# A two-layer hybrid attention trunk on one core: gates' Silu behind the eviction, output banks freed by the copy, gating by two heads of four row tiles, first weights from ScalarE's queue, indexer keys in eights

## What is computed

```python
h = rmsnorm(x, norm_pre)
q, k, v, qi, ki, wi, ga, xb, gb, u, vc, gc = split(h @ w_in)
ya = sparse_attention(...)          # indexer scores relu(qi.ki) weighted by wi, top-k keys, softmax, values
yb = pool_mix(xb)                   # causal windows 2, 4, 8, 16, then a small product and a scale
vn = layernorm(vc); yc = u * (tril(sgu_w[h]) @ vn + sgu_b[h])   # four heads h, chunks of 128 rows
y  = concat([ya * silu(ga), yb * silu(gb), yc * silu(gc)])
x  = x + rmsnorm(y @ w_out, norm_post)
```

## Time and profile before

| | |
|---|---|
| three runs | 1000.95 us median (998.19 to 1001.85) |
| profiled execution | 999.5 us, of which 997.8 us span |
| TensorE (PE) busy | 934.6 us, 94% |
| VectorE (DVE) busy | 535.9 us, 54% |
| ScalarE (ACT) busy | 305.4 us, 31% |
| granted TensorE clock | 0.994 of full speed on average |

### The profile page before, as it was taken

How to read it: one execution, slowest core, us unless ns; L and a number is a source line. 1 busy time by engine, 2 the same in 40 slices (tenths; PEclk the granted TensorE clock), 3 DMA queues, 4 the chain that set the end, 5 groups by cost and what they waited for, 6 DMA issues and landing times.

```text
span 997.8 us, 20531 instructions
## 1 busy us (share of the span) xinstructions
PE 934.6 (94%) x7100; PEld 483.7 (48%) x7100; DVE 535.9 (54%) x1718; ACT 305.4 (31%) x674; POOL 272.6 (27%) x484
## 2 busy tenths in 40 slices
PE   5798999999999999998999999999999999999996
PEld 3434444444454555554555444444445455555543
DVE  4336999475883233233444499966678623332232
ACT  3121121432124245423231211225212424543312
POOL 8710232232222211413342013223222222241110
PEclk9899999999999999999999999999999999999998
DMA  9841677576866655856584338766677667566551
GB/s 314 166 134 43 211 265 250 187 245 226 295 212 212 240 191 186 305 165 222 149 246 128 110 105 280 249 226 207 244 262 246 198 214 249 167 229 247 170 179 53
DMA packets 91954, 205.21 MB, mean 206 GB/s; under 512 B 15047, under 2 KB 26550, under 8 KB 91858
## 3 DMA queue, kind: packets, MB, share of 16 engines
q0 software_dynamic: 38944, 123.98, 36.5%
q1 hardware_dynamic: 47778, 75.78, 23.2%
q10 hardware_dynamic: 5136, 4.20, 1.5%
HBM read 193.88 MB, written 10.14 MB: 204 GB/s over the span
## 4 chain that ended last, share of the span: by engine, by line
PE 74%; DMA 8%; ACT 5%; DVE 4%; issue 4%; ACTq 3%; SPq 1%; POOL 0%; POOLq 0%; DVEq 0%
PE bank L1490 36%; PE bank L1847 10%; PE bank L1507 5%; PE bank L1542 5%; DMA pg<-in_cache_k_dram 4%; PE bank L1473 4%; ACTq L624 2%; PE bank L1723 2%; DMA pg<-in_cache_v_dram 2%; PE bank L1759 2%; PE bank L1591 2%; DMA r<-in_x_prompt_dram 2%; PE bank L1649 1%; PE bank L1565 1%; DVE r L1399 1%
## 5 line engine op out<-in xcount | busy, mean ns | idle before, releaser
L1490 PE MATMUL bank<-wr,ht 128*128 128x512 f32 (+1 forms) x1024 | 436.2, 579 | 5.3 <-DVE ht L1198 2.0
L1490 PEld LDWEIGHTS bank<-wr,ht 128*128 128x128 f32 x1024 | 190.8, 191 | 219.2 <-issue 202.7
L705 POOL DMA_DIRECT2D wr<-in_w_in_dram x50 | 37.1, 742 | 293.0 <-PE bank L1490 225.2
L722 POOL DMA_DIRECT2D pg<-in_cache_v_dram x128 | 69.8, 546 | 165.1 <-PE bank L1542 121.3
L722 POOL DMA_DIRECT2D pg<-in_cache_k_dram x128 | 69.5, 543 | 83.3 <-PE bank L1507 59.2
L1116 DVE TENSOR_SCALAR_CACHE_REDUCE r<-r,sel_i 128x1088 bf16<-128x1088 f32 x62 | 82.8, 1336 | 0.0
L1507 PE MATMUL bank<-pg,qbx 128*32 128x256 f32 x1024 | 63.4, 383 | 7.6 <-DMA pg<-in_cache_k_dram 4.2
L1473 PE MATMUL bank<-wr,ht 128*32 128x256 f32 (+1 forms) x1152 | 65.2, 379 | 2.9 <-DMA wr<-in_w_in_dram 2.6
L1542 PE MATMUL bank<-pg,rs 128*32 128x256 f32 x1024 | 62.3, 382 | 1.8 <-DMA pg<-in_cache_v_dram 1.8
L1847 PE MATMUL bank<-wr,qt 128*128 128x512 f32 x128 | 58.4, 599 | 1.8 <-ACT rs L923 1.8
L1847 PE MATMUL bank<-wr,ht 128*128 128x512 f32 x128 | 57.5, 592 | 0.0
(11 more groups left out here) (271 smaller groups left out, 1167.3 us busy)
## 6 DMA issues: line engine op xcount, KB each, us to landing
pg<-in_cache_k_dram SPq DMA_DIRECT2D x128, 256.0 KB, 5.0
pg<-in_cache_k_dram POOLq DMA_DIRECT2D x128, 256.0 KB, 5.8
pg<-in_cache_v_dram SPq DMA_DIRECT2D x128, 256.0 KB, 5.0
pg<-in_cache_v_dram POOLq DMA_DIRECT2D x128, 256.0 KB, 5.8
wr<-in_w_in_dram POOLq DMA_DIRECT2D x40, 512.0 KB, 4.2
wr<-in_w_in_dram POOLq DMA_DIRECT2D x6, 1024.0 KB, 6.0
...
```

The costliest lines, as they stand in the source:

```text
L705: pool.dma_start(W[n % 2][:, k, d0:d0 + w], src[k.start * P:k.stop * P, c0:c0 + w].rearrange("(k p) n -> p k n", p=P))\
L722: pool.dma_start(PG[2 * gi + e], cache[l, bass.ds(nos[2 * gi + e], 1), :, :].rearrange("o p n -> p (o n)"))\
L1490: mm = pe.matmul(b[0:m, 0:w], HT[:, k, rt * P:rt * P + m], W[n % 2][:, k, 0:w], start=(k == 0), stop=(k == KC - 1))
```

## The change

- **First weights.** ScalarE's own queue issues the weights of chunk kg (two DMAs) before anything else; then it takes one Sqrt of a dummy value, which loads the table that both Square and Sqrt use. GpSimd issues its first 8 keys, waits for these weights, and then issues chunk qi and the constants. The identity's DMA now brings the rotation tables and `query` too, and the cast of the selectors moves to step `wt`.
- **Keys in eights.** A key step of SP and GpSimd loads 8 page numbers and issues 8 DMAs; ScalarE's loads 4 and issues 4. Who brings which keys is dealt anew, and TensorE waits for even and odd quarters apart. On SP tile 2 of x now stands behind 8 keys and tile 3 behind another 8.
- **Order.** `kis` and `whx` go from slot 4 to slot 2; `qis` stays at slot 4 but ahead of that slot's rotation. Chunk q's weights are one DMA behind slot 6. In slots 27, 30, 31, 37 and 39 to 41 `L` goes behind `V`/`K` and `PV`. The last two mask pieces of pair 2 go from slot 30 to the end of slot 29, behind `turn`. `gT` of tiles 1 and 2 go one and two slots back, a `turn` moves from slot 22 to slot 23. `res` and `norm` go to BACK, where they stand behind the key steps of the same slot.
- **Banks.** Chunk xg is copied whole and its bank given back; Silu follows from SBUF behind `P` and `P2`. `out` gives its bank back after the copy, and squares the copy in SBUF.
- **Gating.** `sg` takes two heads of all four prompt tiles at once: two groups of 2 heads x 256 columns in slots 32 and 33.
- **The end.** For the last tile the product with `norm_post` is taken ahead of the root, half by half (`og`), so that one operation is left behind it.

```diff
-KEY_STEPS = [("keys", 1, pair, j) for pair in (0, 1) for j in range(NCH)]
-POOL_KEYS = [("pool keys", 1, pair, j) for pair in (2, 3) for j in range(NCH)]
-TURNS_AT = ((20, 0, 0, (0,)), (20, 4, 0, (1,)), (21, 4, 0, (2,)), (22, 4, 0, (4, 3)),
+SP_KEYS = (((2, 0), (2, 2), (3, 0), (3, 2), (2, 1), (2, 3), (3, 1)), ((2, 0), (3, 0), (2, 2), (3, 2), (2, 1), (3, 1), (2, 3), (3, 3)))
+POOL_KEYS = (((0, 0), (0, 2), (1, 0), (0, 1), (0, 3), (1, 1)), ((0, 0), (0, 2), (0, 1), (0, 3)))
+ACT_KEYS = (((1, 2), (3, 3), (1, 3)), ((1, 0), (1, 2), (1, 1), (1, 3)))
+KEY_STEPS = [[("keys", pair, j, u) for pair, j in ACT_KEYS[l] for u in range(2)] for l in range(DEPTH)]
+def keys_asked(queue, l, odd):
+    return sum(8 for n in range(l + 1) for _, j in queue[n] if j % 2 == odd)
+LOGITS_FIRST = (25, 26, 28, 32, 33, 34, 35, 36, 38)
+TURNS_AT = ((20, 0, 0, (0,)), (20, 4, 0, (1,)), (21, 4, 0, (2,)), (22, 4, 0, (3,)), (23, 0, 0, (4,)),
             (27, 4, 1, (0,)), (29, 4, 1, (1,)), (30, 4, 1, (2,)), (31, 4, 1, (4, 3)),
             (36, 4, 2, (0,)), (37, 4, 2, (1,)), (38, 0, 2, (2,)), (39, 4, 2, (4, 3)),
             (40, 4, 3, (0,)), (41, 4, 3, (1,)), (42, 4, 3, (2,)), (43, 4, 3, (4, 3)))
-MASKS_AT = ((0, (18, 4), (19, 0), 19), (1, (20, 0), (20, 4), 21), (2, (29, 4), (30, 0), 30), (3, (36, 4), (37, 0), 37))
+MASKS_AT = ((0, (18, 4), (19, 0), 19), (1, (20, 0), (20, 4), 21), (2, (29, 0), (29, 4), 30), (3, (36, 4), (37, 0), 37))
...
-        for n, s in zip((1, 2, 2, 3, 3, 4), KEY_STEPS):
-            put(n, BACK, s[:1] + s[2:])
+        for n, s in zip((1, 2, 2, 3, 3, 4), KEY_STEPS[0]):
+            put(n, BACK, s)
...
+    put(at["kg", ST] + 2, FRONT, ("kis",), ("whx",))
+    put(at["qi", ST] + 1, FRONT, ("qis",))
-    put(at["qi", ST] + 1, FRONT, ("kis",), ("whx",), ("qis",))
...
+    for rt in RTP:
+        put(at["xg", rt], ROWS_A, ("silu", "xg", rt))
...
-        put(n, ROWS_A, ("L", i, c))
+        put(n, ROWS_A if n in LOGITS_FIRST else ROWS_B, ("L", i, c))
...
-    for n, rt in enumerate(RTP):
-        put(33 + n, COLS if rt == ST else FRONT, ("sg", rt))
+    put(32, FRONT, ("sg", 0))
+    put(33, FRONT, ("sg", 1))
+    put(37, COLS, ("sg", ST))
+    for rt in RTP:
...
-    for i, n in enumerate((35, 37, 40, 44)):
+    for i, n in enumerate((35, 38, 42, 44)):
...
-            put(46 + n, BACK, KEY_STEPS[n][:1] + KEY_STEPS[n][2:], layer=l + 1)
-        for s, n in zip(POOL_KEYS, (45, 45, 46, 46, 47, 48, 49)):
-            put(n, BACK, s[:1] + s[2:], layer=l + 1)
+            put(46 + n, BACK, KEY_STEPS[l + 1][n], layer=l + 1)
+            put(45 + n, BACK, ("pool keys",) + POOL_KEYS[l + 1][n], layer=l + 1)
     last = {rt: n_out + max(m for m, o in enumerate(OUTS[l]) if o[0] == rt) for rt in RTP}
     for rt in RES[l]:
-        put(last[rt], ROWS_B, ("res", rt))
+        if l + 1 == DEPTH and rt == ST:
+            for j in range(2):
+                put(last[rt] - 1 + j, BACK, ("og", rt, j))
+        put(last[rt], BACK, ("res", rt))
         if l + 1 < DEPTH and rt != 3:
-            put(last[rt] + 1, ROWS_B, ("norm", rt), layer=l + 1)
+            put(last[rt] + 1, BACK, ("norm", rt), layer=l + 1)
...
-        return TILE_ORDER[last + 1:last + 3] if n < NW else TILE_ORDER[last:last + 2]
+        return [TILE_ORDER[last + 1]] if n < NW else TILE_ORDER[last:last + 2]
...
-            for rt in (2, 3):
-                load_keys(sp, mybir.EngineType.SP, 0, 2, 0, ki_in, (rt - 2,))
-                load_rows(rt)
-            load_keys(sp, mybir.EngineType.SP, 0, 2, 0, ki_in, (2, 3))
-            for pair in (3, 0):
-                load_keys(sp, mybir.EngineType.SP, 0, pair, 0, ki_in)
-            load_keys(sp, mybir.EngineType.SP, 0, 1, 1, ki_in, (2, 3))
+            for n, (pair, j) in enumerate(SP_KEYS[0]):
+                load_keys(sp, mybir.EngineType.SP, 0, pair, j, sp_keys_in)
+                if n < 2:
+                    load_rows(2 + n)
...
-            load_w(0, 0)
-            pool.dma_start(cst[:, n_id:], consts[:, n_id:]).then_inc(const_in, 16)
-            pool.dma_start(bits[:, :], bit_table).then_inc(const_in, 16)
-            pool.dma_start(r2[:, 0:2 * P], selectors).then_inc(const_in, 16)
-            load_w(1, 0)
             pool.wait_ge(table_in, 16)
-            for pair in (2, 3):
-                load_keys(pool, mybir.EngineType.Pool, 0, pair, 1, odd_in)
-            load_keys(pool, mybir.EngineType.Pool, 0, 1, 0, odd_in)
+            for n, (pair, j) in enumerate(POOL_KEYS[0]):
+                load_keys(pool, mybir.EngineType.Pool, 0, pair, j, pool_keys_in)
+                if n == 0:
+                    pool.wait_ge(w_first_in, W_IN[0])
+                    load_w(1, 0)
+                    pool.dma_start(cst[:, n_id:], consts[:, n_id:]).then_inc(const_in, 16)
+                    pool.dma_start(bits[:, :], bit_table).then_inc(const_in, 16)
+                    pool.dma_start(r2[:, 0:2 * P], selectors).then_inc(const_in, 16)
...
-                elif name == "xg":
-                    gates = b[NS:2 * NS, 0:DP] if rt == ST else b[:, DP:2 * DP]
-                    copy(ZA[0:m, rt, 0:DP], b[0:m, 0:DP], ACT.Copy)
-                    ins = copy(YP[0:m, rt, :], gates, ACT.Silu)
                 else:
-                    dst = {"qi": ZA, "q": ZA, "k": ZB, "v": V, "uv": ZB, "ga": GA}[name]
+                    dst = {"qi": ZA, "q": ZA, "k": ZB, "v": V, "uv": ZB, "ga": GA, "xg": ZA}[name]
...
-                    nc.scalar.activation(o[:, 256:512], b[NS:2 * NS, 0:256], ACT.Copy).then_inc(o_copied, 1)
-                    act.wait_ge(o_copied, 2 * l + j + 1)
-                    nc.scalar.activation(b[0:NS, :], o, ACT.Square, accum_out=SS[0:m, c:c + 1]).then_inc(act_free, 1)
+                    nc.scalar.activation(o[:, 256:512], b[NS:2 * NS, 0:256], ACT.Copy).then_inc(act_free, 1)
                 else:
-                    nc.scalar.activation(o, b[:, :], ACT.Copy)
-                    nc.scalar.activation(b[:, :], b[:, :], ACT.Square, accum_out=SS[:, c:c + 1]).then_inc(act_free, 1)
+                    nc.scalar.activation(o, b[:, :], ACT.Copy).then_inc(act_free, 1)
+                act.wait_ge(act_free, act_emptied("out", l, rt, j))
+                nc.scalar.activation(JUNK[0:m, 0:512], o, ACT.Square, accum_out=SS[0:m, c:c + 1]).then_inc(o_squared, 1)
+            for piece in CHUNKS[0][1]:
+                c0, w = piece
+                d0 = sum(p[1] for p in CHUNKS[0][1][:CHUNKS[0][1].index(piece)])
+                act.dma_start(W[0][:, :, d0:d0 + w], w_in[0][:, c0:c0 + w].rearrange("(k p) n -> p k n", p=P)).then_inc(w_first_in, 16)
+            act.wait_ge(root_ready, 1)
+            nc.scalar.activation(RSTD[:, 15:16], VAR[:, 15:16], ACT.Sqrt)
...
+                    elif s[2] == "xg":
+                        m, rt = rows(s[3]), s[3]
+                        act.wait_ge(act_free, act_emptied("z", l, "xg", rt))
+                        nc.scalar.activation(YP[0:m, rt, :], ZA[0:m, rt, DP:2 * DP], ACT.Silu).then_inc(silu_done, 1)
...
+                    for e in range(2):
+                        h = 2 * rt + e
+                        u = ZB[:, 0:PT_TILES, h * HD:(h + 1) * HD]
+                        z = b[:, e * 256:(e + 1) * 256].rearrange("p (t d) -> p t d", t=PT_TILES)
+                        ins = nc.vector.scalar_tensor_tensor(u, z, sbt[:, h:h + 1], u, ALU.add, ALU.mult)
+                    own, y = (a[:, 0:PT_TILES, rt * P:(rt + 1) * P] for a in (ZB, YS))
...
+                if l + 1 == DEPTH and rt == ST:
+                    dve.wait_ge(x_back[rt], 16 * (l + 1))
+                    nc.vector.scalar_tensor_tensor(X[rt][0:m, :], OG, RSTD[0:m, 10:11], X[rt][0:m, :], ALU.mult, ALU.add).then_inc(x_new, 1)
+                    return
...
+                if j < 2 and p == 0:
+                    pe.wait_ge(sp_keys_in[j], 16 * keys_asked(SP_KEYS, l, j))
+                    pe.wait_ge(pool_keys_in[j], 16 * keys_asked(POOL_KEYS, l, j))
+                    pe.wait_ge(act_keys_in[j], 16 * keys_asked(ACT_KEYS, l, j))
...
+                        pe.wait_ge(vn_ready, max(done("vn", l, t) for t in range(PT_TILES)))
+                        for e in range(2):
+                            h = 2 * rt + e
+                            mm = pe.matmul(b[:, e * 256:(e + 1) * 256].rearrange("p (t d) -> p t d", t=PT_TILES), WT[:, h, :],
+                                           ZB[:, 0:PT_TILES, DP + h * HD:DP + (h + 1) * HD], start=True, stop=True)
```

110 lines of the change are left out of this document (62 added, 48 removed).

## The result

The changed kernel takes 1006.88 us (median of six runs, 1004.13 to 1011.0), the kernel before 1001.4 us (six runs, 998.19 to 1002.14): ratio 1.0054, 95% interval 1.0034 to 1.0073. So it is 5.5 us slower, where 993.0, faster, was forecast, and it lies above the range, which ended at 1003. The profiled execution has a span of 1004.8 us against 997.8.

The account below looks back on a forecast made before the run. TensorE, busy 934.6 of 997.8 us, was taken as the bound. Terms -8.0 - 2.6 - 10.4 + 10.0 + 3.2 + 6.0 - 4.4 - 1.3 = -7.5 gave 992.0 profiled, 993.0 median; range 980 to 1003.

Parts of the forecast that it names:

- The start: Start of the kernel: `qis` no longer waits 6.45 us, slow clock and a table load go, tile 3's norm later: -8.0 us.
- rival (b): At the start, tile 3 of x lands at 30.4 us, so the start gives only -3: 998.0 us; chance 0.15.
- Chunk q: Slot 8: its wait for the second half of chunk q's weights goes, one DMA being issued earlier: -2.6 us.
- Banks: Both layers: TensorE's waits for banks held by ScalarE, 11.2 us, go but for 0.8: -10.4 us.
- Mask pieces and clock: Pair 2, slots 29 and 30: TensorE stalls for VectorE's select rounds, +10.0 us, and slow clock behind it, +3.2.
- 2.3 us that it takes off for the logit waits: Slot 30 and its like in layer 1: the `L` wait of 1.16 us at 302.09 is won back per layer.
- Change of layer: Slots 46 to 49: ScalarE's key issues stand ahead of norms, `xT` of tile 2 waits 3.4 us: +6.0 us.
- The 1.9 us at kg's bank: Behind the change of layer: the copy of kg's tile 0 comes late for that bank's next product: +1.9 us.
- Gating: `sg` in both layers: fewer, wider groups make TensorE compute less, -2.2 us per layer: -4.4 us.
- The end: Last tile's tail: an operation of 1.22 us and its wait go: -1.3 us.
- Rival (a): Mask pieces of pair 2: the stall does not come, VectorE being in time or the order harmless: 977.5 us; chance 0.10.
- (c): ScalarE's DMA issues slow to SP's rate, 56 issues costing 0.23 us more each, +13: 1006 us; chance 0.12.

Follow-up runs that it names:

- the version without the mask and key losses: Changed kernel with mask pieces back behind slot 30's product, key steps behind the norm, first weights from GpSimd's queue: 982.45 us, ratio 0.9792 to the kernel before.

## Why the prediction was wrong, point by point

- **The start, -8.0: -5.8.** `qis` moved as forecast: no 6.45 us wait, the first `S` at 54.2 against 60.1. Tile 3 of x landed 8.8 us after its issue (15.65 to 24.4), so rival (b) did not come; the rule of the Trainium skill (DMA: Bandwidth & Descriptors, Queues, rings and completion order) that each DMA engine takes the rings in turn had been read as speaking against a second 15 us. The landing agrees with that, but no row shows the taking in turn itself. The table load was worth 1.0 us, not 1.3: from the sample's Square to its `xT` 2.76 us against 3.78. The drain of another 1.38 us that the Trainium skill (ScalarE: Activation LUTs, What ACT_TABLE_LOAD costs) adds does not show in this: here the trace disagrees. The step that failed is that the first weights from ScalarE's queue cost nothing. I named `xT` of tile 0 as their cover and did not ask what they would take from x on the way: that `xT` waited 3.29 us instead of 0.73, and the first product came 2.2 us late. Issued from GpSimd again, they give back 1.1 us of it at the first `S`.
- **Chunk q, -2.6: -2.8**, between the first `S` and slot 8.
- **Banks, -10.4: confirmed in size for the part that was tried.** 6.1 us for a part of 7.1 alone, and 10 us when that part is undone in the version without the mask and key losses, where the waits for the Silu are twice as long. In the changed kernel itself this term cannot be read apart from the gating and the pages.
- **Mask pieces and clock, +13.2: +13.7** between slots 29 and 31 of both layers (6.5 and 7.2), with the waits (13.0) as forecast (12.4) and the product behind at 8.26 and 8.97 against 7.03. The mechanism was named and sized rightly. Only the 2.3 us that it takes off for the logit waits belong elsewhere: the run with the mask pieces back shows that the move of `L` took these away.
- **Change of layer, +6.0: +7.9.** The wait was 4.05 us instead of 3.4, and I left out that the clock falls behind it (2.48 for 1.93). The 1.9 us at kg's bank measured 1.74.
- **Gating, -4.4: nothing.** This is the step that failed most. The computation did shrink, by 3.9 us (8.2 to 4.3 us of busy time), but I took TensorE's busy time as its time. The four groups stood ahead of the pages of slots 33 to 36 and between the xg product and its `P2`. There they covered a fetch and, in the kernel before, the Silu. Two runs from opposite sides show that nothing is won: alone on the kernel before the ratio is 1.0017 (0.9995 to 1.0039, and 4.4 us would be 0.9956), and undone it costs nothing (0.9764 against 0.9792). Where it went is shown in part: alone, in the waits for pages and the Silu, 3.4 us; undone, mostly in the clock.
- **Pages of K and V: no term.** The sum has nothing for them and gives no reason. They were 6.0 us and became 13.0. A page wait is set by when the pages arrive, so what TensorE gains ahead of it, by a shorter computation, a free bank or an `L` out of the way, is partly waited for again. This is the second step that failed.
- **The end, -1.3: -1.3**, from +8.3 at the last output product to +7.0.

Outside the stretches above, the table leaves -4.7 us for banks, gating and pages together, where -14.8 was forecast. So the 14.5 us between -7.5 and +7.0 are: the start 2.2, the mask pieces 0.5, the change of layer 1.9, less 0.2 at chunk q, and 10.1 here, of which 4.4 are the gating. The other 5.7 us lie in the grown waits for pages and in the clock behind them. The runs do not assign them to one part: neither the gating alone (7.7 us of page waits) nor the banks alone (6.9) brings the waits to 13.0, and undoing either in the version without the mask and key losses leaves 12.4 and 12.2. The move of `L`, which the trace points at in slots 39 and 40, was not tried by itself. Between kernels that differ in nothing there, single page waits differ by about 1 us. Why eight pages take over 7 us to arrive (from GpSimd's issues at 337.24 to 344.57 and 346.78) is also open. One cause, the output weights in between, is excluded; the time from a free buffer through the issue was not tried by itself.

No rival named this. Rival (a) asked whether the stall would fail to come, and (c) whether issues would take longer: ScalarE's four took 2.59 us, as before (2.54). The missing rival was that a gain in computation is waited for again, and it had its sign in the earlier trace rows and in the page waits of the kernel before, which I read and did not use.
